# First weight tiles behind two norms run on the un-normalised x, with root and shift applied to their results

## What is computed

```python
def rms_norm(x, g):
    return x * lax.rsqrt(jnp.mean(x * x, axis=-1, keepdims=True) + RMS_EPS) * g

def modulate(h, shift, scale):
    return h * (1 + scale[:, None, :]) + shift[:, None, :]

x = rmsnorm(x, norm_final)                       # end of the first block
mod = jax.nn.silu(c) @ w_ada + b_ada             # shifts, scales, gates of the second
sh_m, sc_m, gt_m, sh_f, sc_f, gt_f = jnp.split(mod, 6, axis=-1)
h = modulate(rms_norm(x, g_mix), sh_m, sc_m)     # norm 0
xin = h @ w_in                                   # first columns: the queries qa
...                                              # attention, mLSTM, @ w_out
x = x + gt_m[:, None, :] * y
h = modulate(rms_norm(x, g_ffn), sh_f, sc_f)     # norm 1
x = x + gt_f[:, None, :] * ((jax.nn.silu(h @ w_gate) * (h @ w_up)) @ w_down)
```

## Time and profile before

| what | value |
|---|---|
| median of 3 runs | 2144.43 us (2141.61 to 2146.88) |
| the profiled execution | 2147.47 us |
| its span | 2145.7 us |
| PE busy | 2111.1 us, 98% of the span |
| DVE, ACT, POOL busy | 1035.3 (48%), 664.4 (31%), 964.1 (45%) us |
| PE's share of the chain that ended last | 94% |

### The profile page before, as it was taken

How to read it: one execution, slowest core, us unless ns; L and a number is a source line. 1 busy time by engine, 2 the same in 40 slices (tenths; PEclk the granted TensorE clock), 3 DMA queues, 4 the chain that set the end, 5 groups by cost and what they waited for, 6 DMA issues and landing times.

```text
span 2145.7 us, 27653 instructions
## 1 busy us (share of the span) xinstructions
PE 2111.1 (98%) x9944; PEld 1721.2 (80%) x9944; DVE 1035.3 (48%) x1657; ACT 664.4 (31%) x874; POOL 964.1 (45%) x712
## 2 busy tenths in 40 slices
PE   7999999999999999999999999998999999999999
PEld 5888778888888878877888888887978677888887
DVE  4577235657473636943547556456254453111111
ACT  4123453312212321244332212133255323212221
POOL 4444334555454544533355455443333124444444
PEclk9999999999999999999999999998999999999999
DMA  5332212334342233221234344322222112222222
GB/s 179 96 103 99 71 68 99 118 137 157 137 156 83 96 112 108 86 96 62 77 118 157 114 151 147 118 99 85 80 85 68 51 40 79 98 99 98 98 98 98
DMA packets 35272, 221.08 MB, mean 103 GB/s; under 512 B 5204, under 2 KB 5588, under 8 KB 9432
## 3 DMA queue, kind: packets, MB, share of 16 engines
q1 hardware_dynamic: 27728, 189.80, 25.6%
q10 hardware_dynamic: 7432, 29.74, 4.0%
HBM read 214.54 MB, written 2.10 MB: 101 GB/s over the span
## 4 chain that ended last, share of the span: by engine, by line
PE 94%; DVE 3%; DVEq 1%; issue 1%; DMA 1%; ACT 1%; SPq 0%; ACTq 0%
PE ps L355 24%; PE ps L357 24%; PE ps L356 24%; PE ps L372 3%; PE ps L374 3%; PE ps L373 3%; PE ps L440 2%; PE ps L402 1%; PE ps L404 1%; PE ps L403 1%; PE ps L461 1%; PE ps L450 1%; DVE yc L1110 1%; PE ps L385 1%; DMA w_raw<-in_weights 1%
## 5 line engine op out<-in xcount | busy, mean ns | idle before, releaser
L326 POOL TENSOR_TENSOR w_lo<-w_raw,w_hi 128x512 fp32r<-128x512 f32 x708 | 963.9, 1393 | 1168.9 <-ACT w_hi L809 1168.9
L355 PE MATMUL ps<-a_hi,w_hi 128*128 128x512 f32 (+2 forms) x1576 | 621.9, 395 | 0.0
L357 PE MATMUL ps<-a_hi,w_lo 128*128 128x512 f32 (+2 forms) x1576 | 614.9, 390 | 0.0
L356 PE MATMUL ps<-a_lo,w_hi 128*128 128x512 f32 (+2 forms) x1576 | 614.6, 390 | 0.0
L809 ACT ACTIVATE w_hi<-w_raw 128x2048 fp32r<-128x2048 f32 x177 | 338.8, 1914 | 778.8 <-PE ps L357 687.9
L355 PEld LDWEIGHTS ps<-a_hi,w_hi 128*128 128x128 f32 (+2 forms) x1576 | 295.0, 187 | 68.7 <-issue 7.3
L357 PEld LDWEIGHTS ps<-a_hi,w_lo 128*128 128x128 f32 (+2 forms) x1576 | 294.8, 187 | 64.5 <-issue 0.8
L356 PEld LDWEIGHTS ps<-a_lo,w_hi 128*128 128x128 f32 (+2 forms) x1576 | 295.1, 187 | 60.9 <-issue 0.6
L355 PE MATMUL ps<-b_hi,w_hi 128*128 128x512 f32 x612 | 239.5, 391 | 0.0
L357 PE MATMUL ps<-b_hi,w_lo 128*128 128x512 f32 x612 | 238.3, 389 | 0.0
L356 PE MATMUL ps<-b_lo,w_hi 128*128 128x512 f32 x612 | 238.1, 389 | 0.0
(11 more groups left out here) (260 smaller groups left out, 2540.6 us busy)
## 6 DMA issues: line engine op xcount, KB each, us to landing
w_raw<-in_weights SPq DMA_DIRECT2D x177, 1024.0 KB, 4.9
v<-in_ada ACTq DMA_DIRECT2D x24, 1024.0 KB, 4.9
x<-in_x_in SPq DMA_DIRECT2D x4, 512.0 KB, 9.6
out<-x SPq DMA_DIRECT2D x8, 256.0 KB, 2.1
bias<-in_mult_bias ACTq DMA_DIRECT2D x1, 640.0 KB
cs_rope<-in_rope ACTq DMA_DIRECT2D x1, 512.0 KB, 7.9
g<-q ACTq DMA_DIRECT2D x16, 32.0 KB, 4.1
g<-k ACTq DMA_DIRECT2D x16, 32.0 KB, 2.1
```

Of the source, the lines that this page charges most:

```text
L326: nc.gpsimd.tensor_tensor(w_lo[:, s, piece], w_raw[:, s, piece], f32(w_hi[:, s, piece]), ALU.subtract).then_inc(w_lo_ready, 1)
L355: nc.tensor.matmul(o, wh, hi(kt), start=kt == 0, stop=False)
L356: nc.tensor.matmul(o, wh, lo(kt), start=False, stop=False)
L357: last = nc.tensor.matmul(o, wl, hi(kt), start=False, stop=kt == depth - 1)
```

## The change

1. **Norm 0 of the second block, first weight block (tiles 0 and 1).** PE runs it on x times a gain, split in the layer before (a new column table `gnext` = final gain x mixing gain x (1 + scale) in the last layer; before, the plain final gain). The sums now stand inside this pair, ahead of x tile 3, and the turns ahead of x tile 6. DVE then multiplies both results by the factor (`first_scales`), ACT adds the shift's share.
2. **The shift's share** is shift^T @ W for the 256 columns: 16 products with two columns (high and low part of the shift) as the stationary side and 256 weight columns moving (`shift_products`), a copy of the 2x256 row by ACT, and two products that turn it into two columns (`shift_columns`).
3. **The second weight block (tiles 2 and 3)** runs high_first on the fully made input. ACT may overwrite a_hi[n] once PE has read it (`first_read`); from n = 3 on it comes behind the shift products, the row's copy and the high part of weight block 2, which has moved there from the first pair's end.
4. **Norm 1** likewise, with b_hi and b_lo as the un-normalised operands, made by ACT and DVE as the x tiles come (`gained_low`); `tail_squares` is gone.
5. **Squares** go to PSUM banks (4 and 5 in turn; banks 2 to 7 at the start) instead of `g`. The squares of q and k go to `yc`, and the four sums of the queries run together behind tile 4.
6. **Start and layer ends.** Silu of c comes ahead of the x tiles; the high part of block 1 comes behind the squares, at the head of the layer loop. In the last chunk of a layer DVE's `low_next` stands ahead of the next tile's addition.

```diff
@@ high_first @@
-            def high_first(o, s, hi_ready, lo_ready, count, low):
+            def high_first(o, s, src, hi_ready, lo_ready, count, low, between={}, read=None):
                 for kt in range(KT):
+                    if kt in between:
+                        between[kt]()
...
+                    if read is not None and kt < KT - 1:
+                        last.then_inc(read, 1)
@@ TensorE, second block @@
+            def shift_products(e, s):
+                pe.wait_ge(shift_split, e + 1)
+                for kt in range(KT):
+                    for w in (w_hi, w_lo):
+                        last = nc.tensor.matmul(ps[7][0:2, 0:2 * P], shift_parts[:, e, kt, :], wcols(w, s, KT, kt, 0, 2 * P),
+                                                start=kt == 0 and w is w_hi, stop=kt == KT - 1 and w is w_lo)
+                last.then_inc(shift_summed, 1)
+
+            def shift_columns(e):
+                pe.wait_ge(shift_row_ready, e + 1)
+                for u in range(2):
+                    last = nc.tensor.matmul(ps[7][:, 2 * P + u:2 * P + u + 1], shift_row[:, u * P:(u + 1) * P],
+                                            ones[0:2, 0:1], start=True, stop=True)
+                last.then_inc(shift_turned, 1)
...
                 if j == 0:
-                    start_pair(0, 0, 0, low)
+                    high_first(banks(0), 0, (a_hi, a_lo), x_hi, x_split, lambda kt: nth(L, 2 * KT, kt), low,
+                               {3: entry_sums, 6: entry_turns}, first_read)
+                    shift_products(0, 0)
+                    continue
+                if j == 1:
+                    high_first(banks(2), 1, (a_hi, a_lo), xm_hi, xm_split, lambda kt: kt + 1, low)
+                    shift_columns(0)
+                    continue
...
-                    if 1 <= t + u <= 8:
-                        qk_sums(t + u - 1)
+                    for r in {AT: range(AT)}.get(t + u, range(t + u - 1, t + u) if AT < t + u <= 2 * AT else ()):
+                        qk_sums(r)
...
-            tail_squares(L)
-            turn_rms(L, 1)
...
                     if j == C_FF:
-                        start_pair(T_FF, j % 2, KT, low)
+                        high_first(banks(t), j % 2, (b_hi, b_lo), xg_hi, xg_split, lambda kt: kt + 1, low,
+                                   {3: lambda: sum_squares(L, 1), 6: lambda: turn_rms(L, 1)})
+                        shift_products(1, j % 2)
@@ ScalarE @@
+            nc.scalar.activation(cs[:, :], sp[:, SP_C:SP_C + KT], ACT.Silu).then_inc(c_silu, 1)
             for n in range(KT):
...
-            w_split(0, 1)
             for n in range(KT):
-                nc.scalar.activation(g[:, n, :], x[:, n, :], ACT.Square).then_inc(x_sq, 1)
-            nc.scalar.activation(cs[:, :], sp[:, SP_C:SP_C + KT], ACT.Silu).then_inc(c_silu, 1)
+                if n == KT - 1:
+                    act.wait_ge(first_used, 1)
+                nc.scalar.activation(first_squared[n], x[:, n, :], ACT.Square).then_inc(x_sq, 1)
...
             with act.Fori(0, LAYERS) as L:
+                w_split(L, 1)
...
+            def modulated(e, shift, block):
                 for n in range(KT):
+                    act.wait_ge(xm_ready, KT * e + n + 1)
+                    if e == 0 and n < KT - 1:
+                        act.wait_ge(first_read, n + 1)
+                    if n == 3:
+                        act.wait_ge(shift_summed, e + 1)
+                        nc.scalar.activation(shift_row, ps[7][0:2, 0:2 * P], ACT.Copy).then_inc(shift_row_ready, 1)
+                        w_split(L, block)
...
-                nc.scalar.activation(g[:, n % 2, :], x[:, n, :], ACT.Square).then_inc(x_sq, 1)
+                nc.scalar.activation(squared[n], x[:, n, :], ACT.Square).then_inc(x_sq, 1)
+                nc.scalar.activation(b_hi[:, n, :], x[:, n, :], ACT.Copy, scale=gs[:, KT + n:KT + n + 1]).then_inc(xg_hi, 1)
@@ VectorE @@
+            def first_scales(e, t, at):
+                nc.vector.tensor_copy(rms[:, :], ps[6][:, :])
+                dve.drain()
+                for u in range(2):
+                    dve.wait_ge(tile_done, nth(L, LAYER_TILES, t + u))
+                    tt(g[:, at + u, :], ps[(t + u) % 4][:, :], rms[:, :], ALU.mult).then_inc(bank_free[(t + u) % 4], 1)
+                    dve.drain().then_inc(first_scaled, 1)
+                dve.wait_ge(shift_turned, e + 1)
+                nc.vector.tensor_copy(shift_col[:, :], ps[7][:, 2 * P:2 * P + 2]).then_inc(shift_ready, 1)
...
+            def gained_low(n):
+                squares(L, n, KT + n)
+                dve.wait_ge(xg_hi, n + 1)
+                nc.vector.scalar_tensor_tensor(b_lo[:, n, :], x[:, n, :], gs[:, KT + n:KT + n + 1], f32(b_hi[:, n, :]),
+                                               ALU.mult, ALU.subtract).then_inc(xg_split, 1)
```

More of the change, by code:

```diff
@@ new lines, in entry_turns @@
+            def entry_turns():
+                pe.wait_ge(rms_spread, nth(L, 2, 0))
+                for tt in range(TT):
+                    last = nc.tensor.transpose(ps[6][:, tt * P:(tt + 1) * P], g[:, 2, tt * P:(tt + 1) * P], ident)
+                last.then_inc(rms_turned, 1)
+                pe.wait_ge(final_spread, 1)
+                for tt in range(TT):
+                    last = nc.tensor.transpose(ps[4][:, tt * P:(tt + 1) * P], g[:, 3, tt * P:(tt + 1) * P], ident)
+                last.then_inc(final_turned, 1)
@@ L969, in _ @@
             L = LAYERS
+            for e in range(2):
+                nc.scalar.activation(shift_parts[:, e, :, 0], mod[:, 3 * KT * e:3 * KT * e + KT], ACT.Copy).then_inc(shift_hi, 1)
             nc.scalar.activation(warm[:, :], ones[:, 0:1], ACT.Sqrt)
@@ L1164, in low, with squares @@
                     squares(L, n, k_, gained)
[L1166 removed]
+            def squares(L, n, k_, gained=False):
                 dve.drain()
                 dve.wait_ge(x_sq, nth(L, 2 * KT, k_))
[L1169 removed]
+                sq = squared[n]
                 if n == 0:
```

153 lines of the change are left out of this document (89 added, 64 removed).

## The result

The changed kernel took 2136.05 us, median of 14 runs (2133.03 to 2141.66), where the kernel before took 2145.65 (14 runs, 2141.33 to 2147.85): a ratio of 0.9955, interval 0.9948 to 0.9963. It is 9.6 us faster. The forecast was 2126.8 with a range of 2119 to 2134, so the direction was right, and the gain was put at nearly twice its size. The profiled execution took 2136.59 (span 2134.5), the profiled one of before 2147.47 (span 2145.7).

The account below looks back on a forecast made before the run. PE was taken to bound the kernel, busy nearly all of the span. Gains of 6.0 (start), 10.7 (norm 0) and 0.9 (norm 1) sum to 17.6: 2147.47 to 2129.9, less 3.0 for the median, 2126.8; range 2119 to 2134.

Parts of the forecast that it names:

- Start, 6.0 forecast: Kernel start, to block 2's first product: 2.8 us from earlier sums and 3.2 behind them, together 6.0 gained.
- the 7 us bound: Start: gain of 7 us if additions take 0.61 us each, where the end of PE's own pair limits.
- The signs: Start: sums expected near 24.5 and block 2's first product near 31.3.
- The cover that I called thin: Start: block 1's low-part quarters ready from 24.5 to 28, each half a microsecond or more before PE uses it.
- Norm 0, 10.7 forecast: Second block's first norm, last product before to query sums' end: 46.8 us falls to 36.1, 10.7 gained.
- rival C: Second pairs bound by the DVE, ACT, DVE chain: 2 us lost at each norm, 2131 to 2133; chance 0.10.
- Behind the query sums, 0 forecast: From the query sums to norm 1: the sum had no term here, so no gain or loss.
- rival E: Clock does not hold through the pairs with thin products among them: half clock costs 44 us, 2171; chance 0.02.
- Norm 1, +0.9 forecast: Norm 1: 1.8 us gained despite a 3.5 us wait, less half of a 1.7 us half-clock cost: 0.9 gained.
- The way to the median: Whole kernel: profiled execution lay 3.0 us above the median, so 2129.9 forecast for it became 2126.8.
- B: Norm 1: DVE backlog holds the pair until 1779 or later, clock falls, 2 to 3 us lost; 2130 to 2131; chance 0.14.
- the prediction's own signs of being wrong: Waits for a_hi or a_lo in second pairs, for w_lo in block 1 at the start, or half clock in a first pair.

Follow-up runs that it names:

- spread_sums: The changed kernel with the four query sums spread in and between the fifth and sixth tiles instead of one row of 32 thin products: 2133.24 us.
- thin_double: The changed kernel with each two-column product of the four query sums issued twice, 64 thin products in a row for 32: 2143.37 us.
- combo: The changed kernel with query sums spread, third block's weight copy behind the modulated tiles, and norm 1's low parts 3 to 7 behind the x updates: 2127.20 us.
- again: The changed kernel run a second time, unaltered, for a second trace and times on the same chip as the others: 2136.33 us.
- late_split: The changed kernel with ScalarE's copy of the third weight block moved, at both norms, from ahead of the fourth modulated x tile to behind the eighth: 2135.01 us.

## Why the prediction was right or wrong

- **Start, 6.0 forecast, 7.2 in the trace.** Mechanism right, the size off by the adds. I took 0.85 for one and it was 0.75, with a reason that fell: PSUM had nothing to do with it, GpSimd's absence had. At 0.75 the adds are done before PE's first pair is, and PE no longer waits: this is the 7 us bound that the sum gave for that case. The signs stood at 24.5 and 31.3 and came at 23.4 and 30.2. The cover that I called thin (block 1's low part) held: PE did not wait.
- **Norm 0, 10.7 forecast, 9.3 in the trace.** First pair, sums, turns, no idleness, shift products (1.83 for 1.9), full clock to the query sums: as priced. The missing 1.4 is the second pair, 12.3 us for 11.0 with 0.3 charged, and the row of sums, 3.63 for 3.2. I had compared the fourth tile's readiness with its use (3.1 against 4.1 us) and found a margin. It was ready at 3.8: ScalarE's list waits for the fourth x tile before it copies the shift row, and stood idle for 0.78 us there. And the copy of 1.9 us also holds VectorE up by 1.35, GpSimd then slows its low parts, and nothing catches up at 1.70 a tile. This is rival C, at 1.3 to 1.4 a norm in place of 2.
- **Behind the query sums, 0 forecast, -3.9 in the trace.** This is the step that failed: the sum ended at the query sums and put what comes behind them at nothing, with no reason given. The clock was checked for the pairs and down to the query sums, where the list of signs ended; that gathering four groups of thin sums into one row of 3.63 us could bring the clock down behind them was a cost of the moved edit that I priced at 3.2 us of work. The evidence cited against rival E was the spacing around the query sums of before, where eight thin products stand alone between tiles, the very thing that the change undid. `spread_sums` and `thin_double` show the row's cost. In its place the traces show about 1.5 us of half clock behind the row, 1.6 for a third stretch in the mLSTM part, and 0.7 of longer waits. That third stretch is seen in six of the seven traces with a fall behind the row and is not explained; `combo` has it without the row.
- **Norm 1, +0.9 forecast, -1.6 in the trace.** The wait was forecast at 3.5 us and was 3.6, ending on the last x update as said. Off were the clock behind it, 1.7 in place of the half of 1.7 that I charged, and the second pair, 12.4 us for 11.0. The 8 slow products that I priced had no row; about 8 came. Taking half of a cost that either comes or does not is a mean, not the likeliest; at a gap of 3.6 us it came in all seven traces that have that gap.
- **The way to the median.** I took 3.0 us off for the profiled execution of before. The profiled one of after lay 0.5 above its own median, so 2.5 us of the miss are from there. The arithmetic: 17.6 - 10.9 (the two profiled times) = 6.7, and 2.5, make the 9.25 between 2126.8 and 2136.05.
- **The range** ended at 2134. It held B and C each alone; both came (B by the clock, its wait was no longer than forecast), and beside them the falls that no case had. Two of the prediction's own signs of being wrong came: half clock in norm 1's first pair, and second pairs held up by a_lo (L408).

## What to carry to other kernels

When short operations are gathered into one row, price the row's effect on the clock of what follows, not only its work: 32 thin products cost 3 to 4 us beyond themselves here, the same ones spread between tiles nothing that can be seen. When an in-order engine gets more work between two results that others wait for, first try the order: eight updates first and five low parts behind them gave 4.3 us for no work saved. And where a copy is placed into a producer's loop, add up what it delays on every engine of the chain per tile, not only the tile it stands ahead of.

## What the runs showed of the hardware

- TensorE's granted clock fell to half with the engine never idle: inside a row of 64 two-column products some 5 us after its begin, and at the end of a row of 32 or just behind it in six traces of eight (in `again` and `late_split` 3 us from its begin, inside the row). The same 32 spread between tiles, 8 or 16 together: full clock in four traces of four.
- A wait of PE of 3.6 us at norm 1 was followed by half clock in seven traces of seven, one of 0.9 us at the same place in none of five.
- Falls that no changed place explains moved between kernels and executions: the 14 times of the changed kernel span 2133.0 to 2141.7, with mean clocks of 0.998 to 0.994.
- A VectorE addition of two SBUF tiles of 128x512 took 0.75 us with GpSimd at rest and 1.22 in the mean with GpSimd at work for 4.5 of the 7.3 us; a low part of two SBUF tiles 0.75 and up to 1.50.
